# First attention of a two-block network: bias and mask of the near keys added on GpSimd, logits and their bound made in one VectorE operation

## What is computed

```python
logits = jnp.einsum("bthd,btkd->bhtk", q_b, k_sel) * (HEAD_DIM ** -0.5)   # 0.125
bias = rel_bias[rel_bucket(t_b[None, :, None] - idx)]
logits = logits + jnp.moveaxis(bias, -1, 1)
logits = jnp.where(valid[:, None], logits, -jnp.inf)
p = jax.nn.softmax(logits, axis=-1)
o = jnp.einsum("bhtk,btkd->bthd", p, v_sel)
```

## Time and profile before

| what | value |
|---|---|
| runs | 2696.7, 2698.06, 2699.41 us; median 2698.06 us |
| profiled execution, its own time | 2696.2 us |
| its span, first to last instruction | 2694.4 us |
| mean granted TensorE clock | 0.973 |
| PE / PEld / DVE busy | 94% / 77% / 64% of the span |
| ACT / POOL busy | 36% / 22% of the span |
| first attention, first logits on VectorE to last values | 521.8 to 685.3 us from the span's start |

### The profile page before, as it was taken

The page is one execution under the profiler, slowest core; times in us unless marked ns, Lnnn a source line. Parts: engine busy times, 40 slices in busy tenths (PEclk is TensorE's granted clock), DMA queues, the critical chain, the costliest instruction groups (busy, mean ns, idle before and its releaser), DMA issues.

```text
span 2694.4 us, 31682 instructions
## 1 busy us (share of the span) xinstructions
PE 2528.4 (94%) x12088; PEld 2082.7 (77%) x12088; DVE 1727.6 (64%) x2928; ACT 972.7 (36%) x1717; POOL 588.8 (22%) x412
## 2 busy tenths in 40 slices
PE   5999999888899899999999999999999988998888
PEld 3778888667787678888888877888778766788877
DVE  5499999488424787787644368568676564008933
ACT  4431222477223322222311243233242244228732
POOL 2247422333443000000000120000000144324333
PEclk7999999899999899999999999999999989999999
DMA  4112233100454265654523132332264115232143
GB/s 165 44 40 63 79 101 100 38 1 9 137 186 135 77 208 173 198 177 140 219 95 109 59 106 79 102 107 82 94 257 156 47 55 165 85 102 68 47 146 102
DMA packets 260705, 293.16 MB, mean 109 GB/s; under 512 B 10856, under 2 KB 216140, under 8 KB 260556
## 3 DMA queue, kind: packets, MB, share of 16 engines
q1 hardware_dynamic: 260556, 291.14, 33.5%
HBM read 223.95 MB, written 66.10 MB: 108 GB/s over the span
## 4 chain that ended last, share of the span: by engine, by line
PE 63%; DVE 28%; ACT 5%; DMA 1%; issue 1%; POOL 1%; SPq 0%; DVEq 0%; ACTq 0%; POOLq 0%
PE ps L67 62%; DVE sm L100 6%; DVE m L97 6%; DVE tmp L103 2%; DVE tmp L79 2%; DVE sm L79 1%; ACT tmp L73 1%; DVE ptl L79 1%; PE ps L70 1%; DVE tmp L76 1%; DVE p2l L76 1%; ACT pth L73 1%; DVE wl L76 1%; DVE X L79 1%; DVE pwa L76 1%
## 5 line engine op out<-in xcount | busy, mean ns | idle before, releaser
L76 POOL TENSOR_TENSOR wl<-raw,wh 128x512 fp32r<-128x512 f32 (+1 forms) x224 | 293.2, 1330 | 1623.6 <-ACT wh L73 1623.5
L73 ACT ACTIVATE wh<-raw 128x512 fp32r<-128x512 f32 (+1 forms) x388 | 226.4, 621 | 257.5 <-PE ps L67 184.7
L73 ACT ACTIVATE tmp<-ps 128x512 f32<-128x512 f32 (+5 forms) x172 | 127.3, 751 | 391.3 <-PE ps L67 379.9
L67 PE MATMUL ps<-B2h,wh 128*128 128x512 f32 x616 | 245.3, 398 | 12.9 <-DVE B2l L76 6.7
L67 PE MATMUL ps<-B2l,wh 128*128 128x512 f32 x616 | 242.5, 394 | 0.0
L67 PE MATMUL ps<-B2h,wl 128*128 128x512 f32 x616 | 242.4, 393 | 0.0
L76 DVE TENSOR_TENSOR tmp<-tmp,ps 128x512 f32<-128x512 f32 x204 | 138.3, 684 | 108.5 <-PE ps L67 92.6
L67 PE MATMUL ps<-ah,wh 128*128 128x512 f32 (+1 forms) x608 | 191.8, 392 | 14.2 <-DVE xt L85 10.2
L73 ACT ACTIVATE wh<-ws 128x512 fp32r<-128x512 f32 x152 | 94.4, 627 | 289.0 <-DVE ws L76 261.9
L67 PE MATMUL ps<-B3h,wh 128*128 128x512 f32 x448 | 178.3, 398 | 15.2 <-DVE B3l L76 7.0
L67 PE MATMUL ps<-al,wh 128*128 128x512 f32 (+1 forms) x608 | 190.4, 390 | 0.0
(11 more groups left out here) (281 smaller groups left out, 5806.8 us busy)
## 6 DMA issues: line engine op xcount, KB each, us to landing
ada<-in_ada_w SPq DMA_DIRECT2D x48, 512.0 KB, 3.9
raw<-in_w_in SPq DMA_DIRECT2D x37, 512.0 KB, 4.4
raw<-in_a_w_in SPq DMA_DIRECT2D x33, 512.0 KB, 4.6
gates<-tmp SPq DMA_DIRECT2D x32, 512.0 KB, 3.0
raw<-in_w_ffn_gate SPq DMA_DIRECT2D x24, 512.0 KB, 6.4
hd<-tmp SPq DMA_DIRECT2D x22, 512.0 KB, 4.5
gf<-hd SPq DMA_DIRECT2D x22, 512.0 KB, 7.2
raw<-in_a_w_out SPq DMA_DIRECT2D x20, 512.0 KB, 3.5
```

What stands on the lines that cost most here:

```text
L67: return self.e.matmul(*a, **k) if self.e else Ins()
L73: return self.e.activation(*a, **k) if self.e else Ins()
L76: return self.e.tensor_tensor(*a, **k) if self.e else Ins()
```

## The change

The bias table is multiplied by 8 when it is made, so that it can be added to unscaled logits. GpSimd, two steps ahead, writes bias plus mask of the near keys into the item's logit buffer. VectorE then needs one `tensor_tensor_reduce` out of PSUM for the near keys: it adds the buffer, writes the logits (now times 8, not scaled, as the far ones were already stored) and carries the minimum of -0.125 x on. `top` is split into `top_far` and `top_near`, and the order of a VectorE step becomes far, norm, near, turned.

```diff
-                    e.tensor_scalar(t, t, self.T1[:, hd * 256:hd * 256 + 1], None, ALU.subtract).then_inc(
+                    e.tensor_scalar(t, t, self.T1[:, hd * 256:hd * 256 + 1], 8.0, ALU.subtract, ALU.mult).then_inc(
...
-        def top(n):
...
+        def top_far(n):
+            W, L, p = (self.ITEMS1[n][0] + 1) * 128, self.LA[n % 7], self.ps(("s", n))
+            far = W - 256
+            if far > 0:
+                e.wait_ge(*self.at("prod", ("s", n)))
+                if n >= 7:
+                    e.wait_ge(*self.at("lfree", n - 7))
+                e.wait_ge(*self.at("mask", self.ITEMS1[n][0]))
+                e.tensor_tensor_reduce(L[:, 0:far], p[:, 0:far], self.SM[self.ITEMS1[n][0]][:, 0:far], -0.125, 3.0e38,
+                                       ALU.add, ALU.min, self.st1(n)[0]).then_inc(vec.up(("far", n)), 1)
+
+        def top_near(n):
...
             e.wait_ge(*self.at("prod", ("s", n)))
+            e.wait_ge(*self.at("near", n))
+            if far:
+                e.wait_ge(*self.at("far", n))
+            e.tensor_tensor_reduce(L[:, far:W], p[:, far:W], L[:, far:W], -0.125, mf if far else 3.0e38,
+                                   ALU.add, ALU.min, mx).then_inc(vec.up(("top", n), ("free", ("s", n))), 1)
...
-            e.scalar_tensor_tensor(out=L[:, far:W], in0=p[:, far:W], scalar=0.125,
-                                   in1=self.T1[:, hd * 256 + 256 - near:hd * 256 + 256], op0=ALU.mult,
-                                   op1=ALU.add).then_inc(vec.up(("near", n), ("free", ("s", n))), 1)
-            e.wait_ge(*self.at("near", n))
-            e.tensor_tensor_reduce(L[:, far:W], L[:, far:W], self.SM[b][:, far:W], -1.0, mf if far else 3.0e38,
-                                   ALU.add, ALU.min, mx).then_inc(vec.up(("top", n)), 1)
...
-        pipeline(64, [(2, norm), (0, top), (4, turned)])
+        pipeline(64, [(0, top_far), (2, norm), (0, top_near), (4, turned)])
...
+        def near(n):
+
+            b, hd = self.ITEMS1[n]
+            W, L = (b + 1) * 128, self.LA[n % 7]
+            far = max(0, W - 256)
             if n < 5:
                 e.wait_ge(*self.at("tfree", self.AT + n - 5))
             elif n >= 7:
                 e.wait_ge(*self.at("lfree", n - 7))
             e.wait_ge(*self.at("mask", b))
...
+            e.tensor_tensor(L[:, far:W], self.T1[:, hd * 256 + 256 - W + far:hd * 256 + 256], self.SM[b][:, far:W],
+                            ALU.add).then_inc(self.sig["gps"].up(("near", n)), 1)
...
+        pipeline(64, [(-2, near), (2, norm)])
```

More of the change, by code:

```diff
@@ L1662, in norm, with turned, pool_attend @@
             e.reciprocal(rs, sm).then_inc(vec.up(("share", n)), 1)
-        def top(n):
-            b, hd = self.ITEMS1[n]
-            W, L, p = (b + 1) * 128, self.LA[n % 7], self.ps(("s", n))
-            near = min(W, 256)
-            far = W - near
+        def top_far(n):
[9 more added lines that the diff above has]
+        def top_near(n):
+            W, L, p = (self.ITEMS1[n][0] + 1) * 128, self.LA[n % 7], self.ps(("s", n))
+            far = max(0, W - 256)
             mf, mx, sm, rs = self.st1(n)
             e.wait_ge(*self.at("prod", ("s", n)))
+            e.wait_ge(*self.at("near", n))
[3 more added lines that the diff above has]
+                                   ALU.add, ALU.min, mx).then_inc(vec.up(("top", n), ("free", ("s", n))), 1)
+        def turned(n):
+            PH, PL, src = self.turned1(n)
+            e.wait_ge(*self.at("ph", n))
+            e.scalar_tensor_tensor(out=PL, in0=src, scalar=1.0, in1=PH.bitcast(F32), op0=ALU.mult,
+                                   op1=ALU.subtract).then_inc(self.sig["vlo"].up(("pl", n), ("free", ("p", n))), 1)
+        pipeline(64, [(0, top_far), (2, norm), (0, top_near), (4, turned)])
+    def pool_attend(self, e):
+        self.pool_zero_v(e, ((self.VE, 64), (self.VLE, 64), (self.VO, 0), (self.VLO, 0)), ("zv1",), [self.PROJECTED])
+        def near(n):
+            b, hd = self.ITEMS1[n]
+            W, L = (b + 1) * 128, self.LA[n % 7]
+            far = max(0, W - 256)
             if n < 5:
@@ L1676, in top, with norm @@
             e.wait_ge(*self.at("mask", b))
-            if far:
-                e.tensor_tensor_reduce(L[:, 0:far], p[:, 0:far], self.SM[b][:, 0:far], -0.125, 3.0e38, ALU.add, ALU.min,
-                                       mf).then_inc(vec.up(("far", n)), 1)
             e.wait_ge(*self.at("t1", hd))
-            e.scalar_tensor_tensor(out=L[:, far:W], in0=p[:, far:W], scalar=0.125,
-                                   in1=self.T1[:, hd * 256 + 256 - near:hd * 256 + 256], op0=ALU.mult,
-                                   op1=ALU.add).then_inc(vec.up(("near", n), ("free", ("s", n))), 1)
-            e.wait_ge(*self.at("near", n))
-            e.tensor_tensor_reduce(L[:, far:W], L[:, far:W], self.SM[b][:, far:W], -1.0, mf if far else 3.0e38,
-                                   ALU.add, ALU.min, mx).then_inc(vec.up(("top", n)), 1)
-        def turned(n):
-            PH, PL, src = self.turned1(n)
-            e.wait_ge(*self.at("ph", n))
-            e.scalar_tensor_tensor(out=PL, in0=src, scalar=1.0, in1=PH.bitcast(F32), op0=ALU.mult,
-                                   op1=ALU.subtract).then_inc(self.sig["vlo"].up(("pl", n), ("free", ("p", n))), 1)
-        pipeline(64, [(2, norm), (0, top), (4, turned)])
-    def pool_attend(self, e):
-        self.pool_zero_v(e, ((self.VE, 64), (self.VLE, 64), (self.VO, 0), (self.VLO, 0)), ("zv1",), [self.PROJECTED])
-        for n in range(0, 64, 2):
-            W, L = (self.ITEMS1[n][0] + 1) * 128, self.LA[n % 7]
-            e.wait_ge(*self.at("share", n))
-            e.tensor_scalar(L[:, 0:W], L[:, 0:W], self.st1(n)[3], None, ALU.mult).then_inc(
-                self.sig["gps"].up(("soft", n)), 1)
+            e.tensor_tensor(L[:, far:W], self.T1[:, hd * 256 + 256 - W + far:hd * 256 + 256], self.SM[b][:, far:W],
+                            ALU.add).then_inc(self.sig["gps"].up(("near", n)), 1)
+        def norm(n):
+            if n % 2 == 0:
+                W, L = (self.ITEMS1[n][0] + 1) * 128, self.LA[n % 7]
+                e.wait_ge(*self.at("share", n))
+                e.tensor_scalar(L[:, 0:W], L[:, 0:W], self.st1(n)[3], None, ALU.mult).then_inc(
+                    self.sig["gps"].up(("soft", n)), 1)
+        pipeline(64, [(-2, near), (2, norm)])
     ATTENDED = (("pv", 31), ("ot", 15), ("pl", 63))
```

## The result

| | before | changed |
|---|---|---|
| median of 20 runs each, us | 2696.79 | 2702.52 |
| lowest to highest, us | 2690.59 to 2702.85 | 2696.26 to 2707.67 |
| profiled execution, us (its span) | 2696.2 (2694.4) | 2702.46 (2700.6) |
| mean granted TensorE clock | 0.973 | 0.973 |

The ratio is 1.002, with a 95% interval of 1.0012 to 1.0028. The change costs 5.7 us, 3 to 8 us by the interval, just past the 0.2% that a measurement of this kernel tells from no change. The forecast was 2705 us, its range 2697 to 2714.

What follows compares the result with a forecast made beforehand. It took the wide half to be bound by the chain from `ptl` over the reciprocal to ScalarE's normalisation. Terms -1.4 + 0 + 8.5 = +7.1 us on 2696.2 gave 2703.3; with the median 1.9 above, 2705 us, range 2697 to 2714.

Steps and rivals of the forecast that it cites:

- What bounds the wide half: First attention, b of 4 and more: in odd steps `ptl`, reciprocal and ScalarE's normalisation form the chain, with no slack.
- The delay, +8.5 us: Wide half, odd steps: the reciprocal waits out the far operation, 0.46 to 0.86 us each; 10.6 less 2.1 us hidden.
- TensorE's own path: Wide half: products, then next logits on TensorE hide part of the delay, 0.75 us over five rounds.
- The saving is worth nothing in the wide half: Wide half: VectorE's cheaper near part gains nothing, because VectorE waits for `pth` afterwards.
- The narrow half, -1.4 us: First attention, b up to 3: gain of 1.4 us at b = 0 and 1; saving and delay cancel at 2 and 3.
- rival B: Whole change: delay half hidden by TensorE, or narrow half gains its full 3 us; no change, 2701 us, chance 0.27.
- The PSUM of the logits, 0 us: End of the near operation: the logits' PSUM comes free as before, within 0.1 us, at no cost.
- The new operation, 0.45 us: VectorE's single near operation out of PSUM: taken as 0.45 us, between rows of 0.412 and 0.485 us.
- GpSimd, 0 us: GpSimd's 64 added additions, 0.81 us each for 128x256: hidden, cost 0.
- A: Rival: VectorE's saving carries the stage, 17 near pieces leave the chain, -7 us, 2691 us; chance 0.08.
- C: Rival: the delay is real and TensorE's clock falls too, +3.4 to +5 us, 2709 us; chance 0.15.
- D: Rival: GpSimd is late and VectorE waits for it, narrow items lose the gain, 2707 us; no chance of its own.

Runs made afterwards that it cites:

- e1: The changed kernel with the reciprocal back in front of the far operation; 2696.41 us, ratio 0.9995 to the kernel before.
- e4: The changed kernel with only the odd items' reciprocals back in front of the far operation; 2692.6 us, ratio 0.9979 to the kernel before.
- e10: The same program as e1, measured again; 2690.79 us, ratio 0.9986 to the kernel before.
- e7: e1 with each of GpSimd's 64 additions issued twice; 2707.15 us, ratio 1.0034 to the kernel before.
- e12: The kernel before with only the odd items' reciprocals moved behind the far operation; 2707.46 us, ratio 1.0036 to the kernel before.
- e3: The changed kernel with the reciprocal still later, behind the near operation; 2720.57 us, ratio 1.0081 to the kernel before.
- e2: The kernel before with only the changed order, all reciprocals behind the far operation, both near operations kept; 2708.46 us, ratio 1.0043.
- e11: The changed kernel itself, measured and profiled once more; 2703.54 us, ratio 1.0025 to the kernel before.
- e6: e1 with ScalarE doing `pth` ahead of its normalisation in each step; 2687.88 us, ratio 0.9967 to the kernel before.
- e8: The kernel before with only ScalarE's order changed, `pth` ahead of the normalisation; 2693.31 us, ratio 0.9989.
- e5: The changed kernel with each reciprocal issued one step sooner, behind the next item's near operation; 2690.27 us, ratio 0.9979 to the kernel before.

## Why the prediction was right, point by point

- **What bounds the wide half.** Right. It named the link from `ptl` over the reciprocal to ScalarE's normalisation, with no slack. Moving only that instruction back takes away 7.4 to 7.8 of the 8.6 us (e1, e4, e10), and 8.2 where the clock is full (e7). Moving only it in the kernel before (e12) makes a loss of 9.5, of which b = 4 has 1.8, in part by the clock.
- **The delay, +8.5 us.** Between the marks 8.6 was measured, where the terms without the last odd step give 8.3, and each block is within 0.6 us of its term. The odd steps grew by what the far operation takes from start to start, in most of them to a few hundredths: 0.62, 0.74 and 0.89 us against the terms 0.60, 0.73 and 0.86. Two grew less, by 0.07 and 0.21 us; for two such the prediction had taken off 0.2. Of the deductions the one for TensorE's own path was too large: it took 0.75 us off, and the long even steps of the last six rounds became shorter by 0.3 us together. b = 4, with 0.84 against 1.4, made up for it.
- **The saving is worth nothing in the wide half.** Right, and shown by e12 against the changed kernel: two near operations or one, the same round to 0.01 us.
- **The narrow half, -1.4 us.** The sign was right, the size not: this is the term that was mis-sized. The profile shows -3.5. I had 2.6 us for the delay and 1.4 + 3.1 for the saving, and set 3.1 and 2.6 equal. Six profiles of kernels with the new operation and ScalarE's old order (e3 and e7 left out) give 46.4 to 50.0 us against 50.95, and the two of the old operations with the changed order (e2, e12) 52.8. Read as they stand, the delay costs some 2 us there and the operation saves some 5, but much of both is TensorE's clock. e1 and e10, one program, differ by 10.4 us at 1.2 GHz and by 3.25 us in time, 0.3 us for each. By this estimate the 3.1 us less at 1.2 GHz of the changed kernel are 1.0 of its 3.5 us, and the clock makes up some 1.6 of the 2 and 2.6 of the 5. What is left of the 3.5, about 2.5 us, lies between my 1.4 and the 3 of rival B. Whether the clock fell less because of the change, and what the kernel before would show in a second profile, no run tells.
- **The sum.** +7.1 forecast, +5.7 measured, +6.3 between the profiled executions. The stage gives -3.5 + 8.6 - 0.8 = +4.3, and the -0.8 is the clock; in e11 it gives -3.7 + 8.6 + 0.6 = +5.5. The other 2 us of the first pair lie ahead of the stage (0.6) and behind it (1.4), in code that did not change. So the closeness of the total is in part luck: the narrow half gave 2.1 us more than forecast, and time outside the stage made up for it. As a number, 2702.5 us lies in the band given to rival B (up to 2703.5) and not in the forecast's own.
- **The PSUM of the logits, 0 us.** It was to come free within 0.1 us of where it did, and comes free 0.3 us later. In the changed kernel this costs the wide half nothing, since e12 with the old operations takes the same steps at b = 5 to 7. It may be what shows in the kernels without the delay: 0.4 us in e7 against the kernel before, 1.4 in e6 against e8.
- **The new operation, 0.45 us.** It takes 0.484, at the upper of the two bounds, because of the scalar it reads (0.412 without) and not because of PSUM. VectorE's busy time therefore fell by 20.8 us, not by the 25 or more that the prediction named as a check.
- **The same rule on PSUM, again.** The new operation reads PSUM and takes 0.484 us; the one of the same width and with the same scalar read SBUF and took 0.485. The Trainium skill ("VectorE: DVE Perf Modes", the section on the TRN2 errata) gives a PSUM source 120 fixed cycles and an SBUF source 58; by an estimate from these 62 cycles the operation should have taken 0.55 us. The trace disagrees for this operation a second time.
- **GpSimd, 0 us.** Right. The addition takes 0.737 us, not 0.81, and nobody on VectorE waits for it. e7 shows how much room there was: none for a second one in the narrow half. On the rule: the Trainium skill ("GPSIMD Engine Reference", section 3.1) says that two-input elementwise work is about twice as slow on GpSimd and belongs on VectorE. The trace agrees on the speed (0.737 us against the 0.42 us of the operation that it replaced), and the runs show that it did not matter, since GpSimd's time was free.
- **The rivals.** A: refuted as it was put, since the delay reached ScalarE by 0.88 us a step and not by less than 0.1. What it would have been worth can be read from e1 and e10, whose order is the old one: by their ratios some 1.3 and 3.8 us faster, by their medians 1.2 and 5.7, not 7. B: the measured ratio lies at its border, and its reason (half of the delay hidden) did not hold. C: the clock in the wide half was 1.00. Whole stretches at 1.2 GHz fell into it in e2 (at b = 4) and e3 alone. D: only with twice the work.
- **The checks it named.** The waits for L88 rose to 15.6 us, above the "about 11": they grew by 10.1 us in the wide half, 1.5 in the narrow one and 1.1 behind the last mark. The estimate left out the waits of the narrow half and took the deductions off as if ScalarE didn't wait in those steps. The waits for `pth` grew by 29 us, more than the work that VectorE saved. The chain shows the far operation and the reciprocal where they were foretold.

## What to carry to other kernels

On an engine that works strictly in order, ask of every instruction who waits for its result and how soon, and put the short ones that another engine waits for ahead of the long ones. A reciprocal of 0.15 us behind a far operation of up to 0.94 us cost more here than a saved operation of 0.42 us in each of 56 items brought. When an edit makes an engine cheaper, look at its order in the same diff as a change of its own, and time the two apart; here the good half alone is 0.05 to 0.2% faster than the kernel before (e1, e10, e4, e5), and turning the other engine's order on top (e6), one line, makes it 0.33%.

## What the runs showed of the hardware

- A VectorE operation with two tensors in SBUF that begins 0.26 us after a GpSimd normalisation takes 0.70 to 1.13 us instead of 0.48, the more the wider the normalisation (e2, each even step of the wide half). With one tensor in PSUM, or begun 0.74 us after a normalisation of 640 keys or 1.0 us after one of 896 (e12), it is not held up. Moving a release on one engine can so slow down an operation on the other that waits for nothing.
- A scalar from SBUF costs this reduction about 0.07 us with a tensor from PSUM (0.412 us without and 0.484 with it, for 128x256) and 0.04 with both from SBUF (0.446 and 0.485).
- An operation on VectorE that reads the result of the reduction ahead of it starts 0.23 us after the read of that result starts (e3: 660.10 and 660.33).
- A two-input addition in fp32 takes GpSimd 0.737 us for 128x256.
- The same program can spend 46.7 or 50.0 us in one stretch, with a granted clock of 0.83 or 0.74 over it. In e10 the runs with a mean clock of 0.970 to 0.972 took 5 to 12 us more than those with 0.973 to 0.977. What decides it between two executions was not found.
